# Reordering the start of the SSD layers: decay rows requested one group after the other, splits and silus in a new order, the first gated tile turned inside the third x unit

## The reference

```python
def ssd_mixer(x, w_in, conv_w, conv_b, dt_bias, a_log, d_skip, norm_w, w_out):
    zxbcdt = x @ w_in
    z = zxbcdt[..., :SSD_D_INNER]
    xbc = zxbcdt[..., SSD_D_INNER:SSD_D_INNER + SSD_CONV_DIM]
    dt_raw = zxbcdt[..., SSD_D_INNER + SSD_CONV_DIM:]
    xbc = jax.nn.silu(depthwise_conv(xbc, conv_w) + conv_b)
    ...
    y_fwd = run_ssd(xs, dt[:, :, 0], a_coef[0], bm, cm)
    y_bwd = flip(run_ssd(flip(xs), flip(dt[:, :, 1]), a_coef[1], flip(bm), flip(cm)))
    y = y_fwd + y_bwd + d_skip[:, None] * xs
    y = y.reshape(bsz, seq, SSD_D_INNER) * jax.nn.silu(z)
    return grouped_rmsnorm(y, norm_w) @ w_out
```

## Time and profile before

| | |
|---|---|
| median of three runs | 1517.72 us |
| profiled execution, its own time | 1520.08 us |
| its span, first to last instruction | 1518.2 us |
| TensorE busy | 1442.0 us (95%) |
| VectorE busy | 997.0 us (66%) |
| ScalarE busy | 768.2 us (51%) |
| GpSimd busy | 196.1 us (13%) |
| mean granted clock of TensorE | 0.981 |

### The profile page before, as it was taken

How to read it: one execution, slowest core, us unless ns; L and a number is a source line. 1 busy time by engine, 2 the same in 40 slices (tenths; PEclk the granted TensorE clock), 3 DMA queues, 4 the chain that set the end, 5 groups by cost and what they waited for, 6 DMA issues and landing times.

```text
span 1518.2 us, 24629 instructions
## 1 busy us (share of the span) xinstructions
PE 1442.0 (95%) x9745; PEld 1331.3 (88%) x9745; DVE 997.0 (66%) x1229; ACT 768.2 (51%) x1104; POOL 196.1 (13%) x245
## 2 busy tenths in 40 slices
PE   6889998999999999999999999999989999899996
PEld 6779997898989989999899889998978999799995
DVE  3889988664567585545754465555778899864545
ACT  3678676353534335444355535443568686454441
POOL 2112322433220000000000000000113222200000
PEclk9899999999999999999999999999989999999998
DMA  7565753566666465555543246555556554446550
GB/s 212 168 194 185 232 167 113 173 195 196 207 203 210 151 213 175 193 196 194 179 157 137 84 139 200 189 188 172 151 191 194 195 172 162 152 167 208 179 209 28
DMA packets 198192, 266.96 MB, mean 176 GB/s; under 512 B 11768, under 2 KB 167824, under 8 KB 198080
## 3 DMA queue, kind: packets, MB, share of 16 engines
q1 hardware_dynamic: 188720, 237.72, 47.5%
q0 software_dynamic: 9200, 27.55, 5.9%
q10 hardware_dynamic: 160, 0.13, 0.0%
HBM read 264.19 MB, written 1.18 MB: 175 GB/s over the span
## 4 chain that ended last, share of the span: by engine, by line
PE 64%; DVE 6%; ACT 3%; issue 2%; DMA 1%; POOL 0%; DVEq 0%; SPq 0%; ACTq 0%; POOLq 0%
PE acc L576 28%; PE y L711 24%; PE acc L597 6%; DVE w_low L1447 2%; ACT w_high L1060 1%; PE y L597 1%; PE inner L856 1%; DMA E<-cumsum_dram 1%; PE inner L677 1%; PE y L974 0%; PE inner L954 0%; DMA raw<-in_ffn_w_out 0%; ACT xT L1090 0%; PE inner L832 0%; DVE xT L1511 0%
## 5 line engine op out<-in xcount | busy, mean ns | idle before, releaser
L576 PE MATMUL acc<-xT,w_high 128*128 128x256 f32 x3264 | 599.6, 285 | 0.0
L1447 DVE TENSOR_TENSOR w_low<-raw,w_high 128x2048 fp32r<-128x2048 f32 (+1 forms) x226 | 511.9, 2274 | 105.7 <-ACT w_high L1060 63.4
L1060 ACT ACTIVATE w_high<-raw 128x2048 fp32r<-128x2048 f32 (+1 forms) x226 | 427.2, 1896 | 206.8 <-PE y L711 77.9
L576 PEld LDWEIGHTS acc<-xT,w_high 128*128 128x128 f32 x3264 | 515.9, 193 | 4.6 <-issue 1.0
L576 PE MATMUL acc<-xT,w_low 128*128 128x256 f32 x1632 | 463.8, 284 | 0.0
L711 PE MATMUL y<-w_high,opT 128*128 128x512 f32 x1408 | 399.3, 393 | 2.8 <-DVE opT L1599 1.4
L576 PEld LDWEIGHTS acc<-xT,w_low 128*128 128x128 f32 x1632 | 315.3, 193 | 0.0
L711 PEld LDWEIGHTS y<-w_high,opT 128*128 128x128 f32 x1408 | 261.0, 189 | 55.2 <-issue 4.2
L711 PE MATMUL y<-w_low,opT 128*128 128x512 f32 x704 | 223.4, 391 | 0.0
L1466 DVE TENSOR_TENSOR opT<-conv,opT 128x512 fp32r<-128x512 f32 x56 | 38.8, 692 | 264.1 <-issue 237.2
L597 PE MATMUL acc<-w_high,xT 128*128 128x256 f32 (+1 forms) x960 | 182.3, 291 | 9.0 <-DVE xT L1511 8.7
(11 more groups left out here) (199 smaller groups left out, 1213.4 us busy)
## 6 DMA issues: line engine op xcount, KB each, us to landing
raw<-in_ffn_w_in SPq DMA_DIRECT2D x128, 512.0 KB, 4.6
raw<-in_ffn_w_out SPq DMA_DIRECT2D x128, 512.0 KB, 4.5
raw<-in_ssd_w_in SPq DMA_DIRECT2D x96, 512.0 KB, 5.3
E<-cumsum_dram POOLq DMA_DIRECT2D x32, 512.0 KB, 6.2
raw<-in_ssd_w_out SPq DMA_DIRECT2D x32, 512.0 KB, 4.4
raw<-in_sc_w_in SPq DMA_DIRECT2D x24, 512.0 KB, 4.7
raw<-in_na_w_qkv SPq DMA_DIRECT2D x24, 512.0 KB, 4.7
raw<-in_sc_w_out SPq DMA_DIRECT2D x8, 512.0 KB, 4.4
```

Of the source, the lines that this page charges most:

```text
L576: mm = nc.tensor.matmul(bank[:, c * SEQ:(c + 1) * SEQ][:, span], w[:, col:col + P], xT[:, k, low, span], start=(k == 0 and part == 0), sto ...
L1060: nc.scalar.activation(w_high[:, u % SPLIT, c0:k * c], raw[:, u % RAW, c0:k * c], ACT.Copy).then_inc(w_high_done, 1)
L1447: V.tensor_tensor(w_low[:, u % SPLIT, c0:k * c], raw[:, u % RAW, c0:k * c], f(w_high[:, u % SPLIT, c0:k * c]), ALU.subtract).then_inc(w_lo ...
```

## The change

GpSimd waits until the decay rows of group 0 have landed before it requests those of group 1, and scales x of group 1 ahead of the power of group 0. On ScalarE, the shift of group 0 is cut in two halves with the tanh of x(0) between; the splits and the copies stand in another order, and the exponents of group 1 stand ahead of a split and the squares. On VectorE, silu(x) stands ahead of the join in groups 0 and 1, splits are moved, and in the pass i == 2 the gate of group 1 comes ahead of a split, the join of group 2 and the taps of bc(2). On TensorE, the gated tile 0 is turned between the two halves of x(2), behind scan(1). No instruction's work is altered, and none is added except the extra wait on GpSimd.

```diff
@@ GpSimd
-                    for g in range(2):
-                        load_decays(g)
+                    load_decays(0)
+                    pool.wait_ge(e_landed[first % 2], 32 * (first // 2 + 1))
+                    load_decays(1)
                     pool.wait_ge(ends_done, first // G + 1)
                     for g in range(G - 2):
-                        scale_xs(g)
+                        if g != 1:
+                            scale_xs(g)
                         own_xs(g)
                         load_decays(g + 2)
+                        if g == 0:
+                            scale_xs(1)
                         rms_power(g)
@@ TensorE, pass i of the loop
                         cross_chunk(i - 1)
+                        scan(i - 1)
                         if i == 2:
 
+                            bank = acc_bank(freed_by("x"))
+                            features(names[("x", i)], bank, range(NT), None, [0])
                             if s:
                                 pe.wait_ge(y_free, 2 * s)
                             turn_gated(0, ring=[("y", 3)])
-                        scan(i - 1)
-                        project(names[("x", i)], range(NT))
-                        if i == 2:
-
+                            used(features(names[("x", i)], bank, range(NT), None, [1]))
                             pe.wait_ge(silu_done, silu_count("z", n0 + 1))
+                        else:
+                            project(names[("x", i)], range(NT))
@@ ScalarE
                     nc.scalar.activation(dtt[:, 2, :, :], dtt[:, 1, :, :], ACT.Exp, scale=-1.0).then_inc(dt_exp, 1)
+                    split_to(first + 4)
                     act.wait_ge(dt_floor, mixer + 1)
                     nc.scalar.activation(dtt[:, 6, :, :], dtt[:, 7, :, :], ACT.Ln).then_inc(dt_log, 1)
-                    split_to(first + 4)
+                    split_to(first + 5)
                     if s:
                         z_tanh(0)
                     z_tanh(1)
-                    split_to(first + 5)
...
-                    split_to(first + 6)
+                    split_to(first + 7)
                     conv_tanh()
                     start_conv("x", 0)
-                    shift_decays(0)
+                    shift_heads(0, early)
                     conv_tanh()
+                    shift_heads(0, late).then_inc(e_shifted, 1)
                     start_conv("bc", 1)
+                    copy_cross(0)
+                    copy_xs(0)
                     decays(0, early)
                     decays(0, late)
-                    copy_cross(0)
-                    copy_xs(0)
                     conv_tanh()
-                    split_to(first + 7)
                     start_conv("x", 1)
@@ VectorE
                     split_to(first + 3)
                     time_constants()
-                    split_to(first + 4)
-                    if s:
-                        silu_z(0)
-                    silu_z(1)
+                    split_to(first + 5)
...
+                    if s:
+                        silu_z(0)
+                    silu_z(1)
                     dve.wait_ge(cs_turned, mixer + 1)
                     V.tensor_copy(csT[:, :], inner_of[("cs_rows", j)][0:2 * HEADS, 0:SEQ]).then_inc(cs_rows, 1)
-                    split_to(first + 5)
-                    silu_bc(0, taps("bc", 0))
+                    y = taps("bc", 0)
                     split_to(first + 6)
+                    silu_bc(0, y)
                     y = taps("x", 0)
                     dve.wait_ge(ends_done, mixer + 1)
+                    silu_x(0, y)
                     join_decays(0)
-                    silu_x(0, y)
                     y = taps("bc", 1)
                     decayed_products(0)
+                    split_to(first + 7)
                     silu_bc(1, y)
-                    split_to(first + 7)
                     y = taps("x", 1)
+                    split_to(first + 8)
+                    silu_x(1, y)
+                    join_decays(1)
                     scale_cross(0)
-                    silu_x(1, y)
-                    split_to(first + 8)
                     add_own(0)
                     gate_scan(0)
-                    join_decays(1)
                     for i in range(2, G - 1):
                         silu_z(i)
-                        if i == 2:
-                            split_to(first + 9)
                         decayed_products(i - 1)
                         if i == 2:
                             split_to(first + 10)
-                        split_to(names[("z", i)] + 4)
-                        join_decays(i)
-                        add_cross(i - 1)
-                        if i == 2:
+                            add_cross(1)
                             gated_low(0)
-                        y = taps("bc", i)
-                        gate_scan(i - 1)
+                            gate_scan(1)
+                            split_to(first + 11)
+                            join_decays(2)
+                            y = taps("bc", 2)
+                        else:
+                            split_to(names[("z", i)] + 4)
+                            join_decays(i)
+                            add_cross(i - 1)
+                            y = taps("bc", i)
+                            gate_scan(i - 1)
                         silu_bc(i, y)
```

More of the change, by code:

```diff
@@ L1147, in conv_tanh, with shift_heads @@
                         tanh_of(conv[:, c % 2, :, :].rearrange("p a b -> p (a b)"), 1.0)
-                    def shift_decays(g):
+                    def shift_heads(g, heads):
                         m = n0 + g
                         act.wait_ge(e_landed[m % 2], 32 * (m // 2 + 1))
-                        for h in range(HPG):
+                        for h in heads:
                             for t in range(NT):
@@ L1157, in shift_decays @@
                                 ins = nc.scalar.activation(e, e, ACT.Identity, bias=apart[:, t, g * HPG + h:g * HPG + h + 1])
-                        ins.then_inc(e_shifted, 1)
+                        return ins
+                    def shift_decays(g):
+                        shift_heads(g, range(HPG)).then_inc(e_shifted, 1)
                     def decays(g, heads):
@@ L1275, in _ @@
                         if i == 2:
+                            decays(1, early)
+                            decays(1, late)
                             split_to(first + 9)
                             squares(0)
-                            decays(1, early)
-                            decays(1, late)
+                            split_to(first + 10)
                             normalise(0)
-                            split_to(first + 10)
-                        split_to(names[("z", i)] + 4)
-                        shift_decays(i)
+                            shift_decays(2)
+                            split_to(first + 11)
+                        else:
+                            split_to(names[("z", i)] + 4)
+                            shift_decays(i)
                         start_conv("bc", i)
```

## The result

The changed kernel took 1527.49 us (median of 5 runs, 1526.47 to 1528.28), the kernel before 1517.72 us beside it (5 runs, 1515.42 to 1521.18). The ratio is 1.0067, 95% interval 1.0055 to 1.0079: some 10 us slower, 3 more than the forecast of 1524.5. The profiled execution was the one of 1527.49 us, with a span of 1525.5.

The account below looks back on a forecast made before the run. TensorE, busy 1442.0 of 1518.2 us, was taken as the bound, its stops set by chains over other engines. Gates +1.8 and clock +5.0 gave +6.8, so 1524.5 us; own range 1521.5 to 1528, full range 1516 to 1529.5.

Parts of the forecast that it names:

- First gate: TensorE's turn of x(0) in each head: silu(x0) at 62.75 and 1107.5, removing stops of 3.75 and 4.15 us.
- S: State products(1), waiting for the bank the gate addition frees: forecast at 82.95 and 1127.7, 3.05 and 4.8 us sooner.
- the trap that the prediction named: Time freed at the turn of x(0) counts only if the next gate, S, moves too.
- Second gate: From silu(x0) to S, set by VectorE's chain: 20.2 us in both heads, with TensorE stopping about 4.1 us at S.
- the port's: VectorE and GpSimd's shared port before S: w_low(7), issued before GpSimd's multiply, takes 2.2 us instead of 3.03.
- Third gate: From S to T: 17.6 us to gated_high plus 13.3 behind it; T 2.45 us later, then 0.65 sooner, sum +1.8.
- T: Turn of gated tile 1 on TensorE, waiting for the normalised gate: forecast at 113.85 and 1158.6, after a 5.9 us stop.
- The faster rival: T opens no stop and comes at S + 25.0, if tanh(bc 2) ends by S + 22: -10.0, 1507.7 us; chance 0.13.
- The clock: Half clock behind the longer stop at T costs TensorE 2.5 us per head, +5.0 in all.
- No change: Rival: clock stays up after S in the first head, only 1.55 paid behind T: +3.5, 1521.2 us; chance 0.22.
- The loss at GpSimd's power: Rival: power(0) falls behind w_low(10), costing a w_low of 2.2 us in both heads: +4.4, 1528.9; chance 0.1.
- the request one by one: Rival: group 0's decay rows land as late as before, silu(x0) at 64.75: +2 per head, 1528.5; chance 0.05.

Follow-up runs that it names:

- asked_together: The changed kernel with the decay rows of both groups requested together again, without the wait between: 1531.68 us, ratio 1.0081 to the kernel before.
- changed_again: The changed kernel run once more, unaltered, with another profile: 1530.4 us, ratio 1.0069 to the kernel before.
- front_only: The kernel before with only the change's edits up to the loop, the pass i == 2 in its old order: 1518.35 us, ratio 1.0001.
- port_free: The changed kernel, but GpSimd fills the two products of group 0 with zeros instead of multiplying: 1525.58 us, ratio 1.004 to the kernel before.
- fill_gap: The changed kernel with split 11 and the join of group 2 ahead of gated_low(0) on VectorE: 1521.73 us, ratio 1.0029 to the kernel before.
- gate_first: The changed kernel with group 1's squares, power and normalising before split 12 and tanh(bc 2), gated_high(0) before split 11, group 2's join before gated_low(0): 1517.67 us, ratio 1.0002.
- before_again: The kernel before the change run and profiled once more, unaltered: 1517.77 us.
- both_gates: gate_first plus group 0's cross scaling, own-token addition and gate ahead of silu(x1) on VectorE, and split 9 ahead of group 1's exponents on ScalarE: 1515.67 us, ratio 0.9975.
- bank_early: both_gates with tanh(bc 2), x(2)'s taps, gated_high(1), gated_low(1) and silu(x2) ahead of split 12, the gated pieces ahead of the silu: 1515.15 us, ratio 0.9973.
- gates_and_x2: both_gates with tanh(bc 2) and x(2)'s first tap ahead of split 12 on ScalarE, silu(x2) ahead of it on VectorE: 1520.05 us, ratio 1.0012.

## Why the prediction was right or wrong

**First gate: right, with less margin than written.** Silu(x0) came at 62.80 (62.75 predicted), and there is no stop before the turn in either head of the first trace. By the rows two things did it: the silu stands ahead of the join, and only half the shift stands ahead of its tanh. The one-by-one request adds about 1 us (asked_together). The prediction said that the decay rows don't hold the silu up; in the second head of changed_again they did. There the shift waited 3.85 us for them, the silu waited 2.50 us for its tanh instead of the 0.94 and 0.80 of the first trace, and the turn stopped 1.68 us. Opened alone, the gate brought no time in the median (front_only) and S stopped 4.66 us: the trap that the prediction named.

**Second gate: right kind, forecast 1.5 us too early.** From silu(x0) to S it took 21.7 us in both heads instead of 20.2. The term that failed is the port's. The prediction asked only which of w_low(7) and the multiply comes first, and had that right (2.28). But the blocked multiply then ran into the silu behind w_low: 1.53 instead of 0.69. And the other multiply had moved: before, it stood beside the state products that VectorE reads from PSUM (inner), and neither was longer than elsewhere (the rows below); with ScalarE's copies moved ahead of the exponents it stands at 66.37, beside the taps, and they took 0.8 more. So +1.6 per head, which port_free takes away. The stops at S were 3.19 and 3.17 us where about 4.1 was written, though S itself was late: TensorE came there at 81.3, not at 78.8, in part because its clock was at 0.50 from 73.8 to 77.2. This shortened the stop and did not move S, which waits for VectorE. The rows of the kernel before for the moved multiply:

```profile
70.71 1.05 POOL L446 TENSOR_TENSOR ring_a<-ring_b,decay_to_end 128x512 f32<-128x512 f32 x1 [14.63 <-ACT ring_b L1187]
```

```profile
71.00 0.29 DVE L1620 SCALAR_TENSOR_TENSOR E<-inner,ident 128x128 f32<-128x128 f32 x1
...
71.21 1.22 DVE L1624 TENSOR_TENSOR E<-E,inner 128x1024 f32<-128x1024 f32 x1
```

**Third gate: right.** From S to T 30.67 and 30.68 us, 30.9 predicted; gated_high at S + 17.5 (17.6), gated_low idle for 4.02 (3.7). fill_gap shows the pieces behind gated_low(0) to be over half of the loss. gate_first takes the whole loss away, with the squares ahead of the tanh, gated_high(0) ahead of a split and the join moved; that the rest is due to the squares alone is likely, not shown. The faster rival fell at its own point: tanh(bc 2) ended at S + 27.8, and it needed S + 22. Between before and after, within each head, T moved by +3.75 and +0.73: +4.5, where +1.8 was predicted; 3.1 of the difference is the error at S, less 0.4 from S to T.

**The clock: wrong by some 4.** Predicted was +2.5 behind each T. The windows after:

```profile
114.80:118.10 3.30, 2.94 (x14) 2.94 (x15) 3.04 (x5) 3.27 (x9) 0.00 (x0) 0.50 0.13 11
1162.70:1169.40 6.70, 3.35 (x16) 3.35 (x17) 4.74 (x7) 6.67 (x19) 0.91 (x2) 0.50 0.09 14
```

The second shows the error: of 6.7 us at granted clock 0.50 (the 1.2 GHz level), TensorE stood still in half. Between T and the next state products, 6.2 us on, the kernel fell 1.35 and 1.51 us further behind, and until the end of the head it took back some 1.0 of each: at the end of the heads the clock behind T had cost 0.3 and 0.5 us, not 5.0 in all. Some 0.4 of what it took back in each head comes at the very end, where the kernel before had a low stretch (258.3 to 261.7 and 1306.2 to 1309.6) and the changed one had none. The same reckoning against the first trace of before gives 0.4 and 1.5 us in changed_again and 1.5 and 1.7 in asked_together: none of these has the 2.5 a head. The prediction took the whole length of a low stretch as run time, from the earlier trace rows, whose windows begin where the stop ends and so hold hardly any of it. The low stretch inside the output unit (104.6 to 107.9) cost nothing, for the stop at T came behind it anyway; it is why that stop was 3.98 us in the first head, not the 5.9 written. In the second head it was 5.46, and 5.55 in the first head of changed_again, where the output unit had no such stretch.

**The rivals.** "No change" had the right idea of a cheap clock in the wrong place: behind S the clock was low in both heads (84.1 to 87.4 in the first) and S to T was the forecast's, while behind T it cost less in the changed kernel's traces than the 1.55 a head that this rival took. The loss at GpSimd's power did not come: the w_low on both sides of it took 2.29 us each. And the request one by one did not leave the silu at 64.75.

**What it didn't see.** Between the heads, where both kernels do the same, the changed one lost 2.0 us more (1074.78 before is 1080.86 after, of which 4.07 were lost by 271.61). No edit lies in this stretch. It lasts 803.2 and 802.9 us in the two traces of the kernel before and 805.2 and 805.8 in the two of the changed one, with single low stretches of the clock at other places. Against the change as its cause stands asked_together, which keeps the change but for one wait: 803.6. All fourteen traces lie between 802.9 and 806.2. Whether the change does it, and how, stays open.

And the median moved by 9.8 while the spans moved by 7.3: the traced run of before was 2.4 over its median. In before_again, near its median, 2 of these are missing at the very start, where the half clock lasted 3.4 instead of 6.8 us. The second pair of traces, before_again and changed_again, lies 13.7 us apart: 2.3 up to the cumulative sums, 4.9 in the first head, 2.9 between the heads and 3.6 in the second.

So the sum came out near (6.8 against 7.3 of span) by parts that cancel: +2.7 at the gates, -4.2 of clock, +2.0 in the middle. That it is so near is luck; that T comes late and costs the time is not.

Of the costs put at nothing: the gated tile turned inside x(2) (98.58) opened no stop, nor did the split before Ln or the z silus show one.

## What to carry to other kernels

A wait removed is worth what the next gate lets through. Here three gates stand in a row, and only kernels that open the last two together (both_gates, bank_early) were faster than the kernel before. On each in-order engine, look for work that stands behind a wait and in front of what a chain needs: moving it into the wait (fill_gap) cost 0.85 us before the output unit and gave back some 6 us in all. Read the releaser in the row before choosing what to hasten: gates_and_x2 hastened the silu though the row named the instruction that frees the bank. And set two traces of each kernel side by side before reading a difference of 2 us.

## What the runs showed of the hardware

A two-input VectorE instruction from SBUF beside a GpSimd multiply took about 0.8 us longer where the two met: w_low 3.03 for 2.28, eight taps 4.05 for 3.26, a silu 1.53 for 0.69. The w_low in which the multiply was issued kept its 2.28, and the silu behind it was the long one, while the multiply showed 3.02 us for some 1.05. A memset of GpSimd (66.92, 0.53 us, within the taps of port_free) lengthened nothing. The Trainium skill (SBUF — State Buffer, Who interferes with whom) says that two SBUF inputs contend with a GpSimd instruction that reads SBUF, and not with one that only writes it; these traces agree.

The granted clock fell in other places in two traces of the same kernel. At S of the second head it was low for 3.4 us in the first trace of the changed kernel (1135.34 to 1138.76, from S on, behind a stop of 3.17) and for 6.8 in the second (1136.17 to 1143.00, of which 2.3 lie in the stop of 4.67 before S at 1138.44); the low stretch inside the output unit of the first (104.52 to 107.93) is missing in the second. One trace's stretch is no fixed price of a stop.
